# The middle of a hybrid decoder layer rewoven: residual stream kept in DRAM, memory norm and gates inside the input projection, two pairs of weight slots, the sample group inside the banded blocks

## The chip, the cores and the metric

The kernel runs on one core of one Trainium2 chip. The metric is the device time of one execution in microseconds (us), median of several runs. TensorE is called PE in the profile, VectorE DVE, ScalarE ACT, GpSimd POOL and SyncE SP. "tile m" below is an output tile of 128 features for all tokens.

## The reference

One decoder layer in float32 (D = 1024) for 1024 prompt tokens and 64 sample tokens (8 sequences of 8), with the same weights; the kernel puts the samples' 64 columns ahead of the prompt's, so T = 1088.

```
x  = x + 0.5 * swiglu(rmsnorm(x, g_ffn1), w1_gate, w1_up, w1_down)     # D_FF = 2816
h  = rmsnorm(x, g_mix);  [u | gate | q | k | v] = h @ w_in             # 512+512+512+128+128
conv = causal depthwise conv of width 4 over u
r, i = sigmoid(block_diag(w_a) conv + b_a), sigmoid(block_diag(w_i) conv + b_i)
a = exp(-8 r softplus(-lam));  b = sqrt(1 - a^2) * i * conv;  h_t = a_t h_{t-1} + b_t
lru_out  = rmsnorm(h * gelu(gate), g_lru_out)
attn_out = rmsnorm(attend(rope(q), rope(k), v, sink), g_attn_out)      # window 128, 8 heads, 2 kv heads
x  = x + concat(lru_out, attn_out) @ w_out
x  = x + softmax((rmsnorm(x, g_xattn) @ w_cq) mk^T / 16) mv @ w_co     # 4 heads, 256 memory tokens
       # prompt: mk, mv = rmsnorm(mem, g_mem) @ w_ck, @ w_cv;  samples: cached mk, mv
x  = x + 0.5 * swiglu(rmsnorm(x, g_ffn2), w2_gate, w2_up, w2_down)
y  = rmsnorm(x, g_final)
```

Besides y the outputs are mk, mv of the prompt, the last keys and values of the window, the convolution's last inputs and the LRU's last states.

## The kernel before

Activations lie with features on the partitions and tokens along the free dimension, in three chunks `CH = [(0, 288), (288, 512), (800, 288)]`. A product of the large weights is made of three matmuls in float32r: hi x hi, hi x lo and lo x hi of operands that are split into a high and a low part (`three`, L552 to L554). ACT writes the high part of activations (`hi_parts`, L1018), VectorE the low part (`lo_parts`, L1315). Weights come in pairs of 128x1024 tiles, 27 in all between the two FFNs (7 of w_in, 8 of w_ck and w_cv in turn, 4 each of w_out, w_cq, w_co), by one DMA per tile on SP's queue (`load_pairs`, L366) into `w_raw[0]` and `w_raw[1]`; GpSimd splits a tile in eight operations of 256 columns (`split_short`, L452 and L453) into the slot's `w_hi`, `w_lo`. There is one such pair of slots.

Input projection. Tile m uses slot m % 2 and PSUM banks 3s, 3s+1, 3s+2, one for each chunk; TensorE starts chunk c of tile m when VectorE has taken that chunk of tile m - 2 (`scaled_take`, L1412, which multiplies by the inverse RMS). VectorE does the convolution of LRU tile ct (L1482, L1489) between the takes of tiles 3 to 7; ACT copies its result over u (L1083). Ahead of tiles 8, 9, 10 and 11 TensorE does six float32 matmuls of the block-diagonal gate weights (`lru_gates`, L737) into banks 6 and 7 in turn, each waiting for ACT's sigmoid (L1092) of the one two before. ACT follows with tanh, exp and square root, VectorE with `lru_gated` (L1501 to L1505) and `lru_scan` (L1511 to L1522); all four LRU tiles share the buffers t_conv, t_a and t_b. ACT's gelu of all gate tiles (L1101) comes with the first of them.

Behind tile 12 come the sum of squares of the LRU output (`sum_squares`, L578), behind tile 13 that of the memory; VectorE does mean, reciprocal (L1302) and the multiplies of the memory norm (L1544), and only then the last take. GpSimd scales the LRU output (L505), four operations of 1088 columns.

Bands. The prompt is worked in eight blocks of 128 tokens. Per block TensorE does the scores (L780), turns the probabilities (`turn_p`, L794), rotates q and k for the block after the next (`rotate`, L768 and L769), does the two tiles of a memory pair (`memory_tile`, L552 to L554 with memn) and weighs the values (`weigh`, L802). VectorE adds the mask (L1587), takes the maxima (L1592), does the rope (L1572 to L1583), takes memory tiles and results out of PSUM (L1277) and normalizes (L1601); ACT does the exponentials (L1119) and copies the turned probabilities (L1131). A memory pair p is multiplied in block p; its weights are split once the pair before has left the slots. The scores of block b+1 are issued at the head of block b. Behind block 6 the samples' rotation, in block 7 their scores, and behind block 7 their turn and weighing (L896, L897) are done, then the attention norm and the output projection.

In SBUF the bands' tables, the rope's buffers and the split memory lie where the split activations `act_hi` and `act_lo` were; x keeps its own 34,816 bytes per partition all the time. The cross attention, its projection and the second FFN follow.

## Time and profile before

| | us |
|---|---|
| median of 3 runs | 2483.44 |
| lowest and highest | 2481.18, 2485.8 |
| the profiled execution | 2480.83 |
| its span (first to last instruction) | 2479.0 |

The span is taken by the hardware profiler. A line of a group names the line of the kernel, the engine and the operation, what it writes and reads, and its shape; behind it stand the busy time and the mean length of one in ns. The idle time in brackets or behind a bar is that of the engine just before the instruction, with what ended it. Matmuls are pipelined, so the length of one is longer than the distance from one to the next: the distance of 0.12 us for 256 columns is what it costs. The granted clock is TensorE's, as a share of 2.4 GHz; 0.5 is 1.2 GHz. The stages: first FFN to 823 us, input projection to 1028, prologue of the bands to 1069, bands to 1217, the samples' tail to 1230, attention norm with the first output tile to 1268, output, query and cross attention to 1670, second FFN and final norm to the end.

### The profile page before, as it was taken

Reading aid. Unit: us, or ns where it says so; the run is one execution under the profiler, and the core shown is the slowest. Engines: PE = TensorE matmul, PEld = TensorE weight load, DVE = VectorE, ACT = ScalarE, POOL = GpSimd, SP = SyncE. Lnnn points to the kernel's source line nnn. Section 1 sums busy time; section 2 is a strip of 40 time slices with the busy share of each in tenths; the row PEclk is TensorE's granted clock in tenths of the full one; section 3 lists DMA queues with packets and bytes.
Section 4 is the critical chain, followed back from the end, with each engine's and each line's share of the span. In section 5 each row is a group of like instructions: output and inputs, shape, how many; then the busy total and the mean of one; then the engine's idle time right before and its main releaser. Section 6 shows DMA issues by size and latency. Waiting matters only on the chain.

```text
span 2479.0 us, 35690 instructions
## 1 busy us (share of the span) xinstructions
PE 2333.8 (94%) x13994; PEld 2070.5 (84%) x13994; DVE 1431.7 (58%) x1864; ACT 444.1 (18%) x908; POOL 1029.9 (42%) x717
## 2 busy tenths in 40 slices
PE   6999999999999999688789989999999999999997
PEld 5899998999998887556578977889998999999896
DVE  7755555655555775876454324447655655565564
ACT  5111100110110416233322013231000000000002
POOL 2543443434433164546635430344434434344333
PEclk9999999999999999899889999999999999999998
DMA  4111101111010010201211134011011110110102
GB/s 142 69 40 45 47 20 51 51 51 51 34 42 26 26 43 26 97 28 58 71 55 48 34 137 170 26 59 69 21 47 51 51 51 35 50 40 28 68 0 74
DMA packets 40285, 131.89 MB, mean 53 GB/s; under 512 B 5799, under 2 KB 11047, under 8 KB 37799
## 3 DMA queue, kind: packets, MB, share of 16 engines
q1 hardware_dynamic: 37280, 127.80, 14.8%
q10 hardware_dynamic: 2951, 3.35, 0.4%
q8 instruction: 36, 0.59, 0.1%
q14 instruction: 18, 0.15, 0.0%
HBM read 123.33 MB, written 7.81 MB: 53 GB/s over the span
## 4 chain that ended last, share of the span: by engine, by line
PE 85%; DVE 6%; POOL 5%; ACT 3%; issue 1%; DMA 1%; POOLq 0%; SPq 0%; DVEq 0%; ACTq 0%
PE ps L552 27%; PE ps L554 26%; PE ps L553 26%; POOL w_hi L452 2%; POOL w_lo L453 1%; PE ps L961 1%; PE ps L914 1%; DVE act_lo L1315 1%; DVE rstd L1302 1%; DVE mem_raw L1544 1%; PE ps L737 1%; PE ps L578 0%; ACT sq L1003 0%; DVE y L1825 0%; ACT act_hi L1018 0%
## 5 line engine op out<-in xcount | busy, mean ns | idle before, releaser
L552 PE MATMUL ps<-act_hi,w_hi 128*128 128x288 f32 (+1 forms) x1968 | 658.0, 334 | 48.0 <-DVE act_lo L1315 34.8
L553 PE MATMUL ps<-act_lo,w_hi 128*128 128x288 f32 (+1 forms) x1968 | 653.1, 332 | 0.0
L554 PE MATMUL ps<-act_hi,w_lo 128*128 128x288 f32 (+1 forms) x1968 | 652.6, 332 | 0.0
L552 PEld LDWEIGHTS ps<-act_hi,w_hi 128*128 128x128 f32 x1968 | 377.5, 192 | 81.9 <-issue 38.6
L553 PEld LDWEIGHTS ps<-act_lo,w_hi 128*128 128x128 f32 x1968 | 377.6, 192 | 29.6
L554 PEld LDWEIGHTS ps<-act_hi,w_lo 128*128 128x128 f32 x1968 | 377.0, 192 | 29.1
L452 POOL TENSOR_TENSOR w_hi<-w_raw,ones 128x256 fp32r<-128x256 f32 x216 | 193.9, 898 | 472.2 <-PE ps L554 440.0
L1358 DVE SCALAR_TENSOR_TENSOR x<-ps,x 128x288 f32<-128x288 f32 (+1 forms) x504 | 263.6, 533 | 188.0 <-PE ps L554 172.8
L552 PE MATMUL ps<-hid_hi,dn_hi 128*128 128x288 f32 (+1 forms) x1056 | 348.7, 330 | 3.6 <-issue 3.6
L554 PE MATMUL ps<-hid_hi,dn_lo 128*128 128x288 f32 (+1 forms) x1056 | 347.7, 329 | 0.0
L553 PE MATMUL ps<-hid_lo,dn_hi 128*128 128x288 f32 (+1 forms) x1056 | 347.7, 329 | 0.0
L552 PE MATMUL ps<-act_hi,up_hi 128*128 128x288 f32 (+1 forms) x1056 | 347.6, 329 | 0.0
L554 PE MATMUL ps<-act_hi,up_lo 128*128 128x288 f32 (+1 forms) x1056 | 347.5, 329 | 0.0
L553 PE MATMUL ps<-act_lo,up_hi 128*128 128x288 f32 (+1 forms) x1056 | 347.5, 329 | 0.0
L1351 DVE TENSOR_TENSOR hid_lo<-hid_t,hid_hi 128x288 fp32r<-128x288 f32 x132 | 329.7, 2549 | 0.4
L443 POOL TENSOR_TENSOR w_hi<-w_raw,ones 128x1024 fp32r<-128x1024 f32 x42 | 102.0, 2428 | 506.8 <-PE ps L554 490.6
L1326 DVE TENSOR_TENSOR gate_t<-ps,rstd 128x288 f32<-128x288 f32 x132 | 70.0, 532 | 375.7 <-PE ps L554 375.1
L443 POOL TENSOR_TENSOR dn_hi<-w_raw,ones 128x1024 fp32r<-128x1024 f32 x22 | 52.9, 2406 | 396.1 <-PE ps L554 325.2
L552 PEld LDWEIGHTS ps<-hid_hi,dn_hi 128*128 128x128 f32 x1056 | 199.9, 189 | 19.2 <-issue 4.0
L554 PEld LDWEIGHTS ps<-hid_hi,dn_lo 128*128 128x128 f32 x1056 | 199.7, 189 | 16.0
L553 PEld LDWEIGHTS ps<-hid_lo,dn_hi 128*128 128x128 f32 x1056 | 200.0, 189 | 15.3
L553 PEld LDWEIGHTS ps<-act_lo,up_hi 128*128 128x128 f32 x1056 | 198.5, 188 | 16.0
(244 smaller groups left out, 2934.3 us busy)
## 6 DMA issues: line engine op xcount, KB each, us to landing
w_raw<-in_w_ffn SPq DMA_DIRECT2D x66, 512.0 KB, 3.7
w_raw<-in_w_plain SPq DMA_DIRECT2D x54, 512.0 KB, 3.6
ff_raw_up<-in_w_ffn SPq DMA_DIRECT2D x44, 512.0 KB, 4.4
ff_raw_down<-in_w_ffn SPq DMA_DIRECT2D x22, 512.0 KB, 6.4
ck_T<-in_ck SPq DMA_DIRECT2D x8, 1024.0 KB, 7.7
cv_n<-in_cv SPq DMA_DIRECT2D x8, 1024.0 KB, 4.9
x<-in_x SPq DMA_DIRECT2D x2, 1152.0 KB, 11.0
x<-in_x SPq DMA_DIRECT2D x1, 2048.0 KB, 12.0
```

Of the source, the lines that this page charges most:

```text
L443: steps.done(pool.tensor_tensor(hi[:, :, :], raw[:, :, :], one, ALU.mult))
L452: steps.done(pool.tensor_tensor(hi[:, r, :], raw[:, r, :], one, ALU.mult))
L453: ins = pool.tensor_tensor(lo[:, r, :], raw[:, r, :], hi[:, r, :].bitcast(F32), ALU.subtract)
L552: pe.matmul(out, wh, ah, start=(first and n == 0), stop=False)
L553: pe.matmul(out, wh, al, start=False, stop=False)
L554: ins = pe.matmul(out, wl, ah, start=False, stop=end)
L737: pe.matmul(ps[:, 6 + n_ % 2, 0:n], bd[:, ct, j // NC, :], mix[:, M_U + ct, o:o + n], start=True, stop=True).then_inc(lru_mm, 1)
L914: pe.matmul(ps[:, h // 2, (h % 2) * NM:(h % 2 + 1) * NM], xq_b[:, 2 * h + d, :], mem_kT[:, 2 * h + d, :], start=(d == 0), stop=(d == 1))
L961: ins = pe.matmul(ps[:, 6 + kt // 4, (kt % 4) * P:(kt % 4 + 1) * P], mem_v[:, mt, kt * P:(kt + 1) * P], xp_T[:, mt, kt // 2, :], start=(mt ...
L1326: dve.tensor_tensor(gate_t[:, o:o + n], ps[:, c, 0:n], rstd[:, o:o + n], ALU.mult)\
L1351: dve.tensor_tensor(hid_lo[s][:, o:o + n], hid_t[:, o:o + n], hid_hi[s][:, o:o + n].bitcast(F32), ALU.subtract).then_inc(f["hid_lo"], 1)
L1358: dve.scalar_tensor_tensor(out=x[:, m, o:o + n], in0=ps[:, DOWN_BANKS[n_ % 8], 0:n], scalar=0.5, in1=x[:, m, o:o + n], op0=ALU.mult, op1=A ...
```

## The change

- The memory's load and norm move to the front of the input projection: the sum of eight squares becomes three adds on VectorE, TensorE's sum comes ahead of tile 3, the multiplies ahead of the take of tile 3.
- x is written to DRAM behind the first FFN (one DMA) and read back in eight (one for each feature tile) behind the last band; the residual add of output tile m waits for its piece. In the meantime the split memory, the tables, the rope's buffers, the convolution's buffer and a second set of t_conv, t_a and t_b lie in its place.
- The gate matmuls of LRU tile ct come chunk by chunk behind the chunks of tiles 5, 7, 8 and 9. VectorE's and ACT's orders are rewritten to fit, with the convolutions in one buffer of their own and the multiply by the gate as a step of its own.
- The first rotation comes inside tile 13; the LRU's reciprocals move behind the first rope, with the takes of tile 13 between them.
- A second pair of weight slots, `kw_hi2[1]` and `kw_lo2[1]`, lies in the place of the activations; memory pair p uses pair p % 2. Pair 0 is multiplied ahead of block 0, pair b+1 in block b, none in block 7. The scores of block b+2 are issued at the end of block b. ACT takes one of a pair's two tiles out of PSUM. The blocks are written out, no longer in a loop.
- GpSimd scales the LRU output in quarters, one tile behind each of the pairs 3 to 6.
- The samples' rotation comes ahead of memory pair 0, their values, scores, turn and weighing behind blocks 0, 1, 3 and 4, in banks 4, 5 and 7.

The diff, cut to its core (buffers first, then SP, GpSimd, TensorE, ACT and VectorE):

```diff
+GATE_TILES = {5: 0, 7: 1, 8: 2, 9: 3}
+        memn_hi = at("memn_hi", [P, KT, NM], X0, F32R)
+        memn_lo = at("memn_lo", [P, KT, NM], X0 + 8192, F32R)
+        TAB0 = X0 + 16384
+        SET0 = (TAB0, P0 + IN_T * ROW)
+        t_conv = [at(f"t_conv{v}", [P, T], SET0[v]) for v in range(2)]
...
+        kw_hi2 = [w_hi2, here("kw_hi2", [P, 2, KT, P], F32R)]
+        kw_lo2 = [w_lo2, here("kw_lo2", [P, 2, KT, P], F32R)]
...
+            sp.wait_ge(f["dn_mm"], FI * NC * KT)
+            sp.dma_start(mem_raw[:, :, :], t_in["mem"]).then_inc(mem_in, 16)
+            sp.wait_ge(f["dn_ev"], 8 + FI * NC * KT)
+            sp.dma_start(t_in["x_keep"], x[:, :, :]).then_inc(x_kept, 16)
             load_pairs(1, 3)
...
+            sp.wait_ge(lru_h, 3)
             for dst, src in ((rotm, "rotm"), (rope_cos, "cos"), (rope_sin, "sin"), (ident, "ident")):
...
+            load_pairs(PAIR_KV + 1, PAIR_OUT + 2)
+            sp.wait_ge(pv_mm, NB)
+            sp.wait_ge(stored, 16 * 7)
+            for m in range(KT):
+                sp.dma_start(x[:, m, :], t_in["x_keep"][:, m, :]).then_inc(x_back[m], 16)
+            load_pairs(PAIR_OUT + 2, PAIR_CO)
...
+            for p in range(1, NB):
+                for s in range(2):
+                    if p == 1:
+                        pool.wait_ge(w_mm[1], groups_before(PAIR_KV))
+                    elif p % 2:
+                        pool.wait_ge(mem_mm, 2 * (p - 2) + 2)
+                    else:
+                        pool.wait_ge(mem_mm, 2 * (p - 2) + s + 1)
+                    split_plain(s, PAIR_KV + p, p % 2)
+                if 3 <= p < 3 + LT:
+                    lru_scale(p - 3)
...
+            def lru_gates(ct, c):
+                if c == 0:
+                    pe.wait_ge(conv_back, ct + 1)
...
+                for w in range(2):
+                    n_ = ct * 2 * NC + 2 * c + w
+                    if n_ >= 2:
+                        pe.wait_ge(lru_ev, n_ - 1)
+                    pe.matmul(ps[:, 6 + w, 0:n], bd[:, ct, w, :], mix[:, M_U + ct, o:o + n],
                               start=True, stop=True).then_inc(lru_mm, 1)
+            for m in range(2, IN_T - 1):
+                if m == 3:
+                    pe.wait_ge(ssq_ev, SUM0["mix"] + NC)
+                    sum_squares("mem", [(0, NM)], 1, mem_sq[:, 0, :])
+                if m in GATE_TILES:
+                    tile("in", m // 2, m % 2, m * NC, after=lambda c: lru_gates(GATE_TILES[m], c))
+                else:
+                    tile("in", m // 2, m % 2, m * NC)
+            pe.wait_ge(lru_ev, 2 * NC * LT)
+            sum_squares("lru", CH, 2 * LT)
...
             def rotate(b):
+                if b:
                     pe.wait_ge(rot_ev, b)
+                    pe.wait_ge(vt_ev, max(b - 1, 1))
+                    pe.wait_ge(kv_ev, max(b * 2 - 1, 3))
...
+            def block_step(b):
+                s = b % 2
+                pe.wait_ge(p_done, b + 1)
...
+                turn_p(b, s, 0)
+                if b + 2 < NB:
+                    rotate(b + 2)
+                turn_p(b, s, 1)
...
+                if b + 1 < NB:
+                    memory_tile(b + 1, 0)
+                weigh(b, 0)
+                if b + 1 < NB:
+                    memory_tile(b + 1, 1)
+                weigh(b, 1).then_inc(pv_mm, 1)
+                if b == 0:
+                    sample_values()
+                elif b == 1:
+                    sample_scores()
+                elif b == 3:
+                    sample_turn()
+                elif b == 4:
+                    sample_weigh()
+                if b + 2 < NB:
+                    scores(b + 2)
+                if b + 1 < NB:
+                    turn_v(b + 1)
+            tile("in", PAIR_KV - 1, 1, (IN_T - 1) * NC, after=rotate_first)
+            pe.wait_ge(g_ev["in"], 6 + 13 * NC + 1)
             scores(0)
+            sample_rotate()
+            pe.wait_ge(memn_lo_done, 1)
+            pe.wait_ge(rot_ev, 1)
+            memory_tile(0, 0)
+            memory_tile(0, 1)
+            pe.wait_ge(g_ev["in"], 6 + 3 * IN_T)
+            turn_v(0)
             rotate(1)
+            scores(1)
...
+            act.wait_ge(mem_in, 16)
+            act.activation(mem_sq[:, :, :], mem_raw[:, :, :], ACT.Square).then_inc(sq_done, 1)
+            rms("mem", [(0, NM)], of=mem_rstd)
+            act.wait_ge(mem_normed, 1)
+            act.wait_ge(x_kept, 16)
+            act.activation(memn_hi[:, :, :], mem_raw[:, :, :], ACT.Copy).then_inc(memn_hi_done, 1)
+            conv_copy(0)
+            for c in range(NC):
+                gates(0, c)
+            conv_copy(1)
+            decay(0)
+            conv_copy(2)
+            input_scale(0)
+            for c in range(NC):
+                gates(1, c)
+            conv_copy(3)
+            decay(1)
+            gates(2, 0)
+            gates(2, 1)
+            input_scale(1)
+            gates(2, 2)
+            decay(2)
+            gates(3, 0)
+            act.wait_ge(g_ev["in"], 6 + 8 * NC)
+            act.activation(mix[:, M_G:M_G + LT, :], mix[:, M_G:M_G + LT, :], ACT.Gelu_apprx_tanh)\
+               .then_inc(gate_gelu, 1)
+            gates(3, 1)
+            gates(3, 2)
+            input_scale(2)
+            decay(3)
+            input_scale(3)
...
+            convolve(0)
+            take_in(4)
+            convolve(1)
+            convolve(2)
+            take_in(5)
+            lru_gated(0)
+            take_in(6)
+            convolve(3)
+            lru_scan(0)
+            take_in(7)
+            lru_gated(1)
+            lru_scan(1)
+            take_in(8)
+            lru_times_gate(0)
+            lru_times_gate(1)
+            lru_gated(2)
+            take_in(9)
+            lru_scan(2)
+            lru_gated(3)
+            take_in(10)
+            lru_scan(3)
+            lru_times_gate(2)
+            lru_times_gate(3)
+            take_in(11)
...
+            rope_read(0)
+            rope(0, 0, steps)
+            for c, (o, n) in enumerate(CH):
+                dve.wait_ge(rms_done, SUM0["lru"] + c + 1)
+                dve.reciprocal(lru_rstd[:, o:o + n], lru_rstd[:, o:o + n]).then_inc(rstd_done, 1)
+                take_in(13, [c])
...
+            def block_step(b):
+                s = b % 2
+                if b + 1 < NB:
+                    add_mask(b + 1, 1 - s, masks[:, 2 - s, :])
+                    if b + 2 < NB:
+                        rope_read(b + 2)
+                    maxima(b + 1, 1 - s, steps)
+                    take_memory(b + 1, 0)
+                    if b + 2 < NB:
+                        rope(b + 2, s, steps)
+                    stage_v(b + 1)
+                    probabilities(b + 1, 1 - s, steps)
+                take_result(b)
...
+                    if stage == "out":
+                        dve.wait_ge(x_back[m], 16)
```

ACT's helpers in the diff: `conv_copy` is the copy of a convolution over u, `gates` the two sigmoids of one chunk, `decay` tanh and exp, `input_scale` the square root. VectorE's `convolve(ct)` waits for `conv_copy(ct - 1)`, since the convolutions now share one buffer.

## Rows read from the trace of the kernel before

**Rows 1.** The page's busy shares: engine, busy us, share of the span, instructions

```profile
PE 2333.8 (94%) x13994; PEld 2070.5 (84%) x13994; DVE 1431.7 (58%) x1864; ACT 444.1 (18%) x908; POOL 1029.9 (42%) x717
```

**Rows 2.** Windows by stage: us, each engine busy, clock, DMA share, GB/s

```profile
826.00:928.00 102.00, 100.71 (x584) 91.21 (x585) 73.38 (x104) 21.15 (x33) 49.95 (x57) 0.97 0.13 42
928.00:1028.50 100.50, 94.14 (x488) 76.00 (x486) 66.54 (x75) 54.96 (x62) 41.97 (x49) 0.97 0.12 38
1028.50:1069.40 40.90, 12.34 (x43) 7.34 (x41) 33.23 (x39) 7.91 (x21) 16.30 (x12) 0.58 0.27 93
1069.40:1217.00 147.60, 122.66 (x779) 87.43 (x779) 98.44 (x138) 50.11 (x152) 98.60 (x115) 0.97 0.20 58
1217.00:1229.70 12.70, 11.04 (x72) 8.82 (x72) 1.02 (x3) 1.06 (x2) 9.79 (x14) 0.69 0.23 61
1229.70:1268.40 38.70, 21.80 (x81) 17.23 (x82) 32.59 (x54) 19.74 (x36) 0.03 (x1) 0.70 0.09 35
```

**Rows 3.** Waits of TensorE, 815 to 1275: us in total, times, longest

```profile
PE ps L768 <- DVE mix L1412: 18.1, 1, 18.1
...
PE ps L552 <- POOL w_lo L453: 17.5, 10, 3.6
...
PE ps L780 <- DVE k_r L1583: 5.2, 2, 4.0
```

**Rows 4.** VectorE in order of time, 892 to 904: start, us, line, operation

```profile
892.03 0.46 DVE L1412 TENSOR_TENSOR mix<-ps,rstd 128x288 f32<-128x288 f32 x1 [0.59 <-PE ps L554]
...
902.44 1.05 DVE L1412 TENSOR_TENSOR mix<-ps,rstd 128x288 f32<-128x288 f32 x2
...
903.96 0.46 DVE L1412 TENSOR_TENSOR mix<-ps,rstd 128x288 f32<-128x288 f32 x1 [0.47 <-PE ps L554]
```

**Rows 5.** TensorE in order of time, first gate group, its first two matmuls

```profile
927.63 1.50 PE L737 MATMUL ps<-mix,bd 128*128 128x288 f32 x4
```

**Rows 6.** VectorE in order of time, reciprocals and memory norm behind the projection

```profile
1015.96 6.96 DVE L1302 RECIPROCAL lru_rstd<-lru_rstd 128x288 f32<-128x288 f32 x3
...
1031.46 13.94 DVE L1544 SCALAR_TENSOR_TENSOR mem_raw<-mem_raw,cst,acc 128x256 f32<-128x256 f32 x8
```

**Rows 7.** GpSimd in order of time, the LRU scale

```profile
1034.62 10.49 POOL L505 TENSOR_TENSOR mix<-mix,lru_rstd 128x1088 f32<-128x1088 f32 x4
```

**Rows 8.** Windows in which the DMA queues are full: keys in, results out

```profile
2472.00:2476.00 4.00, 0.73 (x4) 0.48 (x3) 3.23 (x8) 0.00 (x0) 0.00 (x0) 0.50 1.06 378
...
1466.00:1470.00 4.00, 1.84 (x5) 1.51 (x6) 2.11 (x5) 2.01 (x10) 0.00 (x0) 0.70 0.99 415
```

**Rows 9.** Groups by line and shape, 1069 to 1217: busy us, mean ns

```profile
L452 POOL TENSOR_TENSOR w_hi<-w_raw,ones 128x256 fp32r<-128x256 f32 x58 | 59.1, 1019 | 68.8 <-PE ps L554 68.8
...
L453 POOL TENSOR_TENSOR w_lo<-w_raw,w_hi 128x256 fp32r<-128x256 f32 x57 | 42.4, 743 | 4.5
...
L1119 ACT ACTIVATE s_m<-s_m,st 128x256 f32<-128x256 f32 x56 | 27.7, 495 | 15.6 <-DVE st L1595 15.6
...
L1601 DVE TENSOR_TENSOR s_m<-s_m,st 128x2048 f32<-128x2048 f32 x8 | 20.6, 2575 | 0.3
...
L1587 DVE TENSOR_TENSOR s_m<-ps,masks 128x2048 f32<-128x2048 f32 x7 | 16.0, 2280 | 0.1
...
L1592 DVE TENSOR_REDUCE st<-s_m 128x8 f32<-128x2048 f32 x7 | 15.9, 2273 | 0.0
```

**Rows 10.** TensorE in order of time, two blocks' first turns, a wait between

```profile
1086.42 1.09 PE L794 MATMUL ps<-ident,s_m 128*128 128x128 f32 x8
...
1090.74 0.35 PE L552 MATMUL ps<-w_hi,memn_hi 128*128 128x256 f32 x1 [1.02 <-POOL w_lo L453]
...
1102.77 1.09 PE L794 MATMUL ps<-ident,s_m 128*128 128x128 f32 x8
```

**Rows 11.** GpSimd in order of time, a long operation of a split

```profile
1100.44 2.79 POOL L452 TENSOR_TENSOR w_hi<-w_raw,ones 128x256 fp32r<-128x256 f32 x1
```

**Rows 12.** VectorE in order of time, the first normalizing, GpSimd idle

```profile
1067.02 2.29 DVE L1601 TENSOR_TENSOR s_m<-s_m,st 128x2048 f32<-128x2048 f32 x1
```

More of the change, by code:

```diff
@@ L305, in build @@
         mem_in = sem("mem_in")
+        x_kept = sem("x_kept")
+        x_back = [sem(f"x_back{m}") for m in range(KT)]
         kvc_in = sem("kvc_in")
@@ L690, in ffn_layer, with tile @@
                 last(f)
-            def tile(stage, p, s, n0, feed=None):
+            def tile(stage, p, s, n0, feed=None, after=lambda c: None):
                 pe.wait_ge(w_split[s], p + 1)
@@ new lines, in sample_weigh @@
+            def sample_weigh():
+                pe.wait_ge(s_pt_ev, 3)
+                pe.wait_ge(kv_ev, 2 * 6 + 1)
+                for b in range(NS):
+                    for kv in range(KVH):
+                        t, j = kv * 2 + b // 4, b % 4
+                        r = slice(kv * HD, kv * HD + HD)
+                        out = ps[r, 7, 256 + b * 32:256 + (b + 1) * 32]
+                        pe.matmul(out, v_c[:, b, r], pcs_T[:, t, 32 * j:32 * j + 32], start=True, stop=False)
+                        ins = pe.matmul(out, vs_n[:, b, r], pns_T[:, t, 32 * j:32 * j + 32], start=False, stop=True)
+                ins.then_inc(s_pv_mm, 1)
@@ L1137, in _, with sample_exps @@
+            def sample_exps():
+                act.wait_ge(s_nmax, 1)
+                for t in range(4):
+                    act.activation(ss_m[:, t, :], ss_m[:, t, :], ACT.Exp, bias=st4[:, 1, t:t + 1], scale=HD ** -0.5,
+                                   accum_out=st4[:, 4, t:t + 1])
+                act.activation(st4[:, 3, :], st4[:, 2, :], ACT.Exp).then_inc(s_exp, 1)
             act.sem_inc(pt_ev, 1)
+            take_memory(0, 0)
             exps(0, 0)
             take_v(0, 0)
-            with act.Fori(0, NB // 2 - 1) as i:
-                block_step(i * 2, 0)
-                block_step(i * 2 + 1, 1)
@@ L1691, in _ @@
+            for b in range(NB):
+                block_step(b)
             dve.wait_ge(stored, 16 * 7)
@@ L1725, in plain_residual @@
                     take(s, pair0, s)
-                with dve.Fori(1, KT // 2) as i:
-                    for s in range(2):
-                        take(i * 2 + s, i + pair0, s)
+                if stage == "out":
+                    for i in range(1, KT // 2):
+                        for s in range(2):
+                            take(i * 2 + s, i + pair0, s)
+                else:
+                    with dve.Fori(1, KT // 2) as i:
+                        for s in range(2):
+                            take(i * 2 + s, i + pair0, s)
                 dve.wait_ge(g_ev[stage], 6 + NC * KT)
```

574 lines of the change are left out of this document (269 added, 305 removed).

## The prediction

> **What bounds the kernel now.** The page's busy shares come first [rows 1]: TensorE is busy in 94% of the span. So matmuls bound the kernel wherever they are fed, and a change that takes few of them away can win only in holes. The windows by stage [rows 2] show how large these are. The first half of the input projection (826 to 928) has 1.3 us of TensorE idle; the half with the gates (928 to 1028.5) has 6.4; the prologue of the bands (1028.5 to 1069.4) has 28.6 of 40.9, at a mean granted clock of 0.58, so mostly at the 1.2 GHz level; the eight bands (147.6 us) have 24.9; the sample group's tail takes 12.7 us at 0.69; the norm after it has 16.9 of 38.7. The waits of TensorE [rows 3] name the holes that are reached here: 18.1 us for the last tile's take, which on VectorE stands behind the memory norm; 17.5 us in ten waits for GpSimd's weight splits; 5.2 us in two waits of the scores for the rope.
>
> **Input projection, tiles 8 to 13.** A tile takes 11.93 us (its take to that of the next [rows 4]). 100.5 us for six tiles leaves 100.5 - 71.6 = 28.9 us for the four gate groups, the LRU sums and stalls. Of a gate group's six matmuls the first two (chunks of 288 and 512) take 1.50 us [rows 5]; a third of 288 adds about 0.5, so six cost 4.0 (bounds 3.0, and 6.6, which is all of the 28.9 less the sums). Spread over three chunks they don't wait for sigmoids: the bank that each needs was emptied a chunk (3 to 5 us) ago. Four groups: 16.0. The LRU sums stay at an estimated 2.6; a memory sum of 0.5 and a rotation of 1.1 are new here. 28.9 - 20.2 = 8.7, of which stalls get 1.7: **7 us** (bounds 0 and 12).
>
> The stalls would come from VectorE's order. convolve(2) waits for ACT's copy of tile 1, which now stands behind the gates of tile 5, and the take of tile 5 stands behind convolve(2). A convolution with its copies is 9.9 us (892.5 to 902.4 [rows 4]). Tile 5 starts at 892, its gates end at 908, ACT has copied by 910, the convolution ends at 920, and tile 7 wants the bank at 920: under 1 us lost. Later VectorE waits some 7 us for the gelu, which stands on ACT behind the first gates of tile 9. As a load: VectorE had 73.4 + 66.5 us in both halves [rows 2]; 7.0 of reciprocals [rows 6] go to the prologue, the memory norm adds about 14: 147 in 192 us. Followed in order, it ends the adds for the LRU sums at 1000, and TensorE wants them at 1002.6. This slack of 3 us carries the part.
>
> **The memory norm.** Its eight multiplies took 13.94 us [rows 6], while GpSimd ran splits and the LRU scale [rows 7] without a gap. Now they lie in tile 3, beside at most one split: I take 7 us (0.9 each; bounds 3 and 14), and 2.3 each for the three adds in place of the reduction, for mean and reciprocal, and for the low part. Tiles 2 to 4 cover all of it, since VectorE has only 1.4 of takes in each 11.9 us there; without that cover the convolutions start later by as much and the 3 us are gone.
>
> **x to DRAM and back.** 4.46 MB each way. The queues moved 415 GB/s in and 378 GB/s out [rows 8], so 11 to 12 us, behind 3 us for the memory's 1 MB. The write starts at 827 with the last take, ends at about 842, and the weights of pair 1, queued behind it on SP, land by 845. Their slot is free at 842, TensorE needs the split at 856, a split is 6 us: 5 us remain. Cost 0 (bounds 0 and 5). The way back starts with the end of the last band, 1.5 us for each of eight pieces; the first output tile is taken over 20 us later, and the weights behind it on the queue (the third pair) are wanted later still. Cost 0.
>
> **Prologue.** Gone are the 18.1 us and the slow work behind them. After tile 13 (at about 1020 now) VectorE is still at the reciprocals with the takes between them; it starts on the scores about 3 us after the last matmul. Then one chain: mask 2.3, maximum 2.3 and small ones 0.6, eight exponentials of 0.5, the turn of the values 0.6, rotation 1.3 and rope 2.6 for block 1 (behind the exponentials, since the rotation waits for the copy of the first values; the rows bound a rope by 4.0 [rows 3]), normalizing 2.9 [rows 9]: 16.6. With 1 us for the clock, the first turn is 20.5 us after tile 13 and no longer 40.9: **20.4 us** (bounds 14 and 25). The sample's rope lies beside the exponentials, memory pair 0 in a hole of TensorE.
>
> **Bands.** From one block's first turn to the next's is 16.35 us, of which 1.02 is a wait for GpSimd [rows 10]: 15.3 us where the weights are there in time. Yet eight blocks took 147.6 us, as the next pair's split had to wait for the slots of the last. With two slot pairs GpSimd starts a block ahead. Now: block 0 with a cold clock 15.5, and its scores 2.2; six blocks 91.8, less 3.0 of rotation and scores that have no successor; block 7, without a memory pair, 7.6; the sample's four pieces 12 (the tail's 12.7 [rows 2] less its waits, plus its scores); friction 3. Sum 129: **18 us** (bounds 5 and 24).
>
> What must keep up. GpSimd: sixteen operations a pair, 1.02 on average for one half and 0.74 for the other [rows 9], are 14.1 us, 11.8 without VectorE's company; at shorter blocks I take 15.3. Four blocks add an LRU scale of 2.65 [rows 7]. From 1025: 12.5 + 6 x 15.3 + 10.6 = 115, pair 7 is ready at 1140; TensorE wants it 5.4 us into the turns of block 6, at 1148. VectorE: mask, rope read, maximum, exponentials and normalizing of the next block are 15.5 us from its scores, and TensorE comes for them after 17.1: 1.6 us of slack.
>
> **The sample's tail.** The 12.7 us between the last band and its result [rows 2] go, a take of 0.7 stays: **12 us** (bounds 9 and 12.7). The norm behind it keeps its chain and its cold clock.
>
> **Sum.** 7 + 20.4 + 18 + 12 = 57.4. The profiled execution took 2480.83 us (span 2479.0 and 1.8 around it), 2.6 under the median of the runs. 2480.8 - 57.4 + 2.6 = **2426 us**.
>
> **A rule against it.** One operation of GpSimd takes 2.79 us, where the mean of its line is 1.02 [rows 9, 11], and normalizing 2.58 on average [rows 9] where it takes 2.29 with GpSimd idle [rows 12]. The Trainium skill, "SBUF — State Buffer", section "SBUF: two separate sides", says that a VectorE operation with two SBUF inputs and a GpSimd operation take one port pair in turn, each for its whole length. By that rule, the trace agrees in these rows, a pair would cost GpSimd its 11.8 and VectorE's 4.2 of such work (2.3 of normalizing, the rest rope), 16.0, and pair 7 would come at 1144, still 4 us ahead: the sum stays.
>
> **Rivals.**
> First, VectorE sets the pace of the bands. For it: a slack of 1.6 us, and GpSimd now splits in all of a block and not in two thirds (98.6 of 147.6 [rows 2]); some nine operations of VectorE in a block read SBUF twice and can each meet one of 0.73, 0.4 on average, so 3.3 to 3.6 us, 2 beyond the slack. Against: 12.3 us of VectorE's work in 15.3. Over seven blocks 14 us: 2440. GpSimd at 17 us a pair would give the same.
> Second, the input projection turns into a convoy: each take of tiles 5 to 12 is late by 2 us behind a convolution or a scan. For it: VectorE and ACT each wait for the other in a strict order. Against: 147 in 192 us. The 7 us go and 8 more: 2441. Both together: 2455.
> Third, slower: the write of x runs far below the rate of the rows. The weights of tile 2 are behind it, and so is the memory's high part. The write has 12 + 5 us before TensorE waits; all beyond that is TensorE idle, and it eats the gain above 75 us, so under 60 GB/s. At 50 GB/s (89 us) it costs 72: 2498. For it: no row shows 4.46 MB in one write. Against: 378 GB/s of output [rows 8].
>
> **How the numbers follow.** The forecast has 0.63 (its own range 2417 to 2435), the first rival 0.17, the second 0.12, both together 0.04, the third 0.03, no change at all 0.01. Downward, 2411 holds 5 us more in the prologue, 6 in the bands and 4 in the projection, out of their bounds; upward both single rivals are in, with 9 us on top for the prologue's upper price: 2450. About 0.2% (5 us) can be told from no change. Faster 0.96, same 0.01, slower 0.03.
>
> **What would show it.** Tile 13 ends near 1020, the first turn comes near 1040; from one block's first turn to the next's 15 to 16 us, with no wait for GpSimd above 1 us; the last band ends near 1168, output tile 0 near 1207; the DMA share is near 1 for 12 us after 828. Wrong would be: waits of the projection's tiles for VectorE's takes over 5 us in all (second rival), a wait for the normalized scores in every block (first), a hole ahead of tile 2 (third).

## The result, and the profile after

The changed kernel takes 2420.55 us (median of four runs, 2418.85 to 2422.93), the one before 2482.44 us beside it: ratio 0.975, 95% interval 0.9738 to 0.9761, faster. The forecast was 2426 us, its range 2411 to 2450. On another chip the changed kernel took 2421.56 us (five runs, ratio 0.9754, interval 0.9741 to 0.9768).

The profiled execution has a span of 2417.1 us, 61.9 less than before. First the line of busy shares of its page; the line before is [rows 1].

```profile
PE 2317.7 (96%) x13994; PEld 2064.9 (85%) x13994; DVE 1432.2 (59%) x1858; ACT 449.6 (19%) x918; POOL 1052.5 (44%) x729
```

Just as many matmuls, but 16.1 us less of TensorE's busy time (its mean granted clock is 0.983, before 0.973); the rest of the gain, some 46 us, is holes. The windows by stage of the changed kernel (columns as in [rows 2], whose first four and last lines they answer):

```profile
826.00:928.00 102.00, 100.76 (x570) 89.95 (x571) 79.99 (x110) 36.45 (x49) 50.93 (x55) 0.97 0.27 96
928.00:1017.50 89.50, 89.50 (x506) 77.40 (x504) 73.79 (x91) 44.44 (x49) 60.54 (x50) 1.00 0.17 55
1017.50:1041.40 23.90, 14.96 (x91) 11.74 (x90) 19.55 (x27) 5.97 (x20) 21.09 (x25) 0.79 0.41 132
1041.40:1168.70 127.30, 121.55 (x801) 87.00 (x799) 98.03 (x123) 53.67 (x161) 107.08 (x127) 0.96 0.24 69
1168.70:1207.60 38.90, 20.73 (x74) 16.06 (x75) 32.38 (x52) 19.85 (x36) 0.00 (x0) 0.78 0.34 132
```

Against [rows 2] the second half of the projection is 11.0 us shorter, the prologue 17.0, the bands 20.3, and the samples' tail of 12.7 is gone; the norm behind it is 1.1 longer (output tile 0 is taken 38.8 us after its start, 37.7 before). That makes 59.9 of the 61.9. The last lines of this section say where most of the other 2 lies.

The waits of TensorE from tile 13's end to the last band (line, waited for, us in total, times, longest); they answer [rows 3]:

```profile
PE ps L819 <- DVE k_r L1711: 4.8, 1, 4.8
PE ps L835 <- ACT p_T L1235: 3.2, 3, 1.4
PE ps L829 <- DVE mem_kT L1390: 3.2, 1, 3.2
PE ps L581 <- issue: 2.3, 2, 1.2
PE ps L581 <- POOL w_lo L478: 0.6, 1, 0.6
```

The wait for the last tile's take (18.1) is gone, of 17.5 us for GpSimd 0.6 is left. What stays is one 4.8 us wait for a rope, and one of 3.2 for a memory tile that VectorE takes late. The 0.6 lies in the prologue; in the bands TensorE never waits for GpSimd. The two waits put down to "issue" (1.24 us at 1078.12 and 1.10 at 1094.38, ahead of the memory pairs in blocks 2 and 3) are VectorE's as far as the order shows: `block_step` waits there for `rot_ev`, and VectorE's last reading of that rotation ends at 1078.01 and 1094.27; one experiment's profile names it at this place (`DVE rot_k`, 1.4 us). VectorE in the prologue, in order of time (start, us, line, operation):

```profile
1026.31 0.42 DVE L1756 TENSOR_TENSOR rot_q<-ps,rope_sin 128x256 f32<-128x256 f32 x1
...
1029.54 0.41 DVE L1390 TENSOR_SCALAR mem_kT<-ps 128x256 f32<-128x256 f32 x1
1033.34 0.69 DVE L1700 TENSOR_TENSOR rot_q<-ps,rope_sin 128x512 f32<-128x512 f32 x1 [3.39 <-PE ps L808]
...
1036.10 1.17 DVE L1710 TENSOR_TENSOR q_r<-q_r,rot_q 128x512 f32<-128x512 f32 x1
1037.19 0.81 DVE L1711 TENSOR_TENSOR k_r<-k_r,rot_k 128x128 f32<-128x128 f32 x1
...
1038.34 2.47 DVE L1729 TENSOR_TENSOR s_m<-s_m,st 128x2048 f32<-128x2048 f32 x1
```

The samples' rope (1026.31 to 1029.6) stands ahead of the take that TensorE needs; then VectorE itself waits 3.39 us for the rotation, whose matmuls run at the low clock; then come the rope and the normalizing. The late take costs nothing, though. The rotation waits for ScalarE's copy of the first values, and that copy stands directly behind the exponentials, when the turn of the values (1030.10 to 1030.40) is already done:

```profile
1030.47 0.26 ACT L1219 ACTIVATE v_n<-ps 128x128 f32<-128x128 f32 x1
...
1030.83 2.04 PE L807 MATMUL ps<-mix,rotm 128*128 128x512 f32 x2 [0.43 <-ACT v_n L1219]
```

The write of x, in windows, first the kernel before, in which nothing is written, then the changed one:

```profile
830.00:840.00 10.00, 10.00 (x50) 8.95 (x49) 9.26 (x16) 8.98 (x15) 0.00 (x0) 0.86 0.00 0
```

```profile
830.00:840.00 10.00, 10.00 (x50) 8.91 (x49) 9.29 (x16) 9.00 (x16) 0.00 (x0) 0.87 0.99 385
840.00:850.00 10.00, 9.57 (x56) 8.03 (x55) 8.64 (x9) 5.77 (x7) 5.82 (x8) 1.00 0.23 73
```

385 GB/s from SBUF to DRAM, and TensorE, VectorE and ScalarE as busy beside it as without it: no hole ahead of tile 2. The memory's multiplies, in tile 3, took 5.28 us in place of the 13.94 of [rows 6].

The last 2 us: in the last product of the kernel, behind a stop of 2.05 us that both have, TensorE of the kernel before fell to its lower level for seven matmuls (0.43 apart, later 0.23), that of the changed one did not. Before, then after:

```profile
2446.70 1.14 PE L640 MATMUL ps<-y_id,lrup 96*128 96x96 f32 x6 [2.05 <-DVE lrup L1820]
2447.55 0.78 PE L552 MATMUL ps<-hid_hi,dn_hi 128*128 128x512 f32 x1
```

```profile
2386.45 0.91 PE L669 MATMUL ps<-y_id,lrup 96*128 96x96 f32 x6 [2.05 <-DVE lrup L1975]
2387.14 0.48 PE L581 MATMUL ps<-hid_hi,dn_hi 128*128 128x512 f32 x1
```

Nothing there was changed. That is about 1.5 us of clock, and no property of the change: in the second profile of the changed kernel, with a span of 2418.6, the same matmuls run at the low level again. The rest, some 0.5 us, is not followed up.

### The profile page after: what moved, and what is told of

Its sections match the earlier page's. It is cut to its first block, busy times and chain, and to the rows that moved or that the text cites. A ratio compares the mean times of both kernels' runs of the same rounds, so it can differ in the third digit from the quotient of the medians.

```text
span 2417.1 us, 35425 instructions
## 1 busy us (share of the span) xinstructions
PE 2317.7 (96%) x13994; PEld 2064.9 (85%) x13994; DVE 1432.2 (59%) x1858; ACT 449.6 (19%) x918; POOL 1052.5 (44%) x729
## 4 chain that ended last, share of the span: by engine, by line
PE 92%; DVE 4%; ACT 2%; POOL 1%; issue 1%; DMA 0%; ACTq 0%; SPq 0%; DVEq 0%; POOLq 0%
PE ps L581 28%; PE ps L582 28%; PE ps L583 28%; PE ps L981 1%; PE ps L843 1%; PE ps L1028 1%; DVE act_lo L1428 1%; PE ps L819 1%; PE ps L769 1%; DVE rstd L1415 1%; PE ps L607 1%; PE ps L835 1%; ACT sq L1070 0%; ACT act_hi L1085 0%; DVE y L1980 0%
## 5 line engine op out<-in xcount | busy, mean ns | idle before, releaser
L583 PEld LDWEIGHTS ps<-act_hi,w_lo 128*128 128x128 f32 x1968 | 377.2, 192 | 28.9
L477 POOL TENSOR_TENSOR w_hi<-w_raw,ones 128x256 fp32r<-128x256 f32 x184 | 162.7, 884 | 388.4 <-PE ps L583 356.6
L468 POOL TENSOR_TENSOR w_hi<-w_raw,ones 128x1024 fp32r<-128x1024 f32 x42 | 101.9, 2426 | 507.9 <-PE ps L583 491.7
L582 PEld LDWEIGHTS ps<-hid_lo,dn_hi 128*128 128x128 f32 x1056 | 199.9, 189 | 15.1
L581 PEld LDWEIGHTS ps<-act_hi,up_hi 128*128 128x128 f32 x1056 | 198.9, 188 | 15.9
```

Of the source, the lines that this page charges most:

```text
L468: steps.done(pool.tensor_tensor(hi[:, :, :], raw[:, :, :], one, ALU.mult))
L477: steps.done(pool.tensor_tensor(hi[:, r, :], raw[:, r, :], one, ALU.mult))
L581: pe.matmul(out, wh, ah, start=(first and n == 0), stop=False)
L582: pe.matmul(out, wh, al, start=False, stop=False)
L583: ins = pe.matmul(out, wl, ah, start=False, stop=end)
```

## The experiments

All times are medians. "The changed kernel" is 2420.55 us; "the changed kernel beside it" is its run on another chip, 2421.56, together with two of the experiments ("More work for GpSimd" and the first kernel of "The prologue in another order"). The length of a block is taken from the second half of its first turn to that of the next block's. No experiment takes back the prologue's 17.0 us alone, with the memory norm and the take of tile 13: that part is read from the two traces only.

### One weight slot pair

```diff
-        kw_hi2 = [w_hi2, here("kw_hi2", [P, 2, KT, P], F32R)]
+        kw_hi2 = [w_hi2, w_hi2]          # kw_lo2 likewise
...
-                    elif p % 2:
-                        pool.wait_ge(mem_mm, 2 * (p - 2) + 2)
+                    if p % 2:
+                        pool.wait_ge(mem_mm, 2 * (p - 1) + s + 1)
```

> The changed kernel (2420.6 us), with the second weight slot pair taken away: all memory pairs are split into the first pair of slots, each as soon as the matmuls that read its predecessor are through. Theory (the forecast's term for the bands): the eight bands were stretched by waits for GpSimd's splits alone, 17.5 us in ten waits in the kernel before. They come back: 15 to 20 us, so 2436 to 2441 us, first turn to end of last weighing about 144 us in place of 127. Rival: the gain in the bands came from the new order of the blocks (written out, rotation two blocks ahead, samples inside); then under 5 us come back, below 2426 us.

Measured: 2440.98 us, ratio to the kernel before 0.9833 (0.9817 to 0.985): 20.4 us come back. Its waits for GpSimd:

```profile
PE ps L579 <- POOL w_lo L478: 14.6, 6, 6.3
```

The slot pair is what the bands' gain hangs on, and the rival (the new order) is out. 14.6 is waiting. Part of the rest is the clock: block 4, with the weighing in it, takes 35.3 us in place of 26.7, though its wait is 6.3; over the bands the granted clock is 0.90 there and 0.96 in the changed kernel.

### Gate groups in one piece

```diff
-                    tile("in", m // 2, m % 2, m * NC, after=lambda c: lru_gates(GATE_TILES[m], c))
+                    tile("in", m // 2, m % 2, m * NC)
+                    for c in range(NC):
+                        lru_gates(GATE_TILES[m], c)
```

> The changed kernel with each LRU gate group in one piece behind its tile, no longer two matmuls behind each chunk. Theory: a group in one piece waits for the sigmoids of its first chunks; four groups took 28.9 us less 2.6 of sums in the kernel before, 6.6 us each, against 3.6 woven: 10 to 12 us come back, 2431 to 2433 us. Rival: the projection's gain came from VectorE's order and from the memory norm being gone there; then un-weaving costs under 3 us, about 2423 us.

Measured: 2434.99 us, ratio 0.9811 (0.9795 to 0.9827): 14.4 us, a little above the theory's 10 to 12. TensorE in order of time at tile 9's group, the last, and the stage's waits:

```profile
966.89 1.13 PE L769 MATMUL ps<-mix,bd 128*128 128x288 f32 x4
969.47 1.98 PE L769 MATMUL ps<-mix,bd 128*128 128x512 f32 x4 [1.44 <-ACT t_a L1167]
977.00 2.29 PE L769 MATMUL ps<-mix,bd 128*128 128x288 f32 x4 [5.55 <-ACT t_a L1167]
```

```profile
PE ps L769 <- ACT t_a L1167: 8.4, 3, 5.5
```

The wait of 5.55 is ScalarE's order: the gelu stands behind the first gates of the last group, and the rest of that group waits for it. Woven in, a chunk of large matmuls lies between. 8.4 us of waits, four groups of 4.75 in place of 4.1 and a clock of 0.97 in place of 1.00 make up the difference. Without the weaving none of the projection's gain (11.0) is left. The 14.4 is not the weaving's worth alone, though: 5.5 of it is an order of ScalarE that was made for woven groups and stayed here.

### The samples behind the last band

```diff
-                if b == 0:
-                    sample_values()
-                elif b == 1:
-                    sample_scores()
...
+            sample_values()
+            sample_scores()
+            sample_turn()
+            sample_weigh()      # behind the last block; ScalarE and VectorE likewise
```

> The changed kernel with the four sample pieces (values, scores, turn, weighing) in one chain behind the last band. Theory: the matmuls (about 12 us in the blocks) only move, but each piece now waits for VectorE or ScalarE: mask and maxima, exponentials, normalizing, copies, with a falling clock. 10 to 14 us more, 2431 to 2435 us. Rival: the pieces cost in the blocks what they cost behind them, the same matmuls being only moved: under 3 us, about 2423 us.

Measured: 2436.06 us, ratio 0.9814 (0.9797 to 0.983): 15.5 us more, the theory's side and a little above its 10 to 14. The windows of bands, samples and norm:

```profile
1042.00:1161.20 119.20, 110.08 (x658) 78.21 (x657) 97.96 (x113) 50.05 (x149) 109.59 (x127) 0.96 0.25 72
1161.20:1184.00 22.80, 15.21 (x145) 12.00 (x144) 3.77 (x10) 3.84 (x12) 0.00 (x0) 0.63 0.01 2
1184.00:1222.50 38.50, 20.02 (x76) 15.47 (x75) 32.05 (x51) 19.78 (x36) 0.00 (x0) 0.73 0.34 133
```

and of its waits:

```profile
PE ps L582 <- POOL kw_lo L479: 5.7, 2, 5.0
PE ps L892 <- DVE ss_m L1772: 5.3, 1, 5.3
```

Two things are to be seen. The tail costs 22.8 us, 10 more than the one of [rows 2], which had part of its work beside block 7. And the bands become only 8.1 us shorter, though the pieces are gone from them: without them blocks 0 to 3 take 15.0 to 15.3 us each, and then TensorE waits 5.0 us for pair 7. At 15.0 us a block GpSimd doesn't keep up: in the changed kernel the splits of a pair take it 12.0 to 15.1 us, 14.0 on average, and the four LRU scales between pairs 3 and 7 another 16.1 in all. The samples' pieces in the blocks, above all the weighing in block 4, give it the time.

### The write of x three times

```diff
+            for i in range(2):
+                sp.dma_start(t_in[f"x_keep{i}"], x[:, :, :]).then_inc(x_kept, 16)
             sp.dma_start(t_in["x_keep"], x[:, :, :]).then_inc(x_kept, 16)
```

> The changed kernel with the write of x made three times (to three tensors in DRAM, one behind the other on the same queue), 34.8 us in place of 11.6. Theory (slower rival of the forecast): the write may take 17 us before TensorE waits for the weights behind it, all beyond is idle TensorE: 18 us more (13 to 23), 2434 to 2444 us, with a hole ahead of tile 2. Rival: the three writes overlap or the weights are not held up by them; then under 5 us.

Measured: 2434.61 us (2431.02 to 2439.19), ratio 0.9809 (0.9791 to 0.9827): 14.0 us. TensorE's waits for GpSimd's splits, this one and the prologue's 0.6:

```profile
PE ps L583 <- POOL w_lo L480: 13.6, 2, 13.0
```

One hole of 13.0 us ahead of tile 2, where the theory had 18 and named the range from 13. 23.2 us of writes were added, so the slack behind the single write was some 10 us, where the theory had 17 - 11.6 = 5.4. The slower rival of the forecast is real as a mechanism; by this estimate it decides from about 22 us of write on, and the write takes 11.6.

### More work for GpSimd

```diff
+                for i in range(4):
+                    pool.tensor_tensor(pool_pad[:, :], memn_hi[:, 0, :].bitcast(F32), ...).then_inc(pad_done, 1)
+                    pool.wait_ge(pad_done, (p - 1) * 4 + i + 1)
```

> The changed kernel with four more GpSimd multiplies of 128x256 elements behind each memory pair's split (results unused), each waited for: some 3.5 us a pair. Theory: GpSimd runs without idle, but ahead of TensorE: pair 7 is ready at 1139 and wanted at about 1154, 15 us of slack; six additions of 3.5 are 21, so some 6 us (2 to 10) come out, 2423 to 2431 us. Rival (the forecast's first, GpSimd paces the bands): every addition counts, 20 to 25 us, 2441 to 2446 us. Third way: lock or port contention with VectorE lengthens each block by about 1 us more: 8 us on top.

Measured: 2429.95 us, ratio 0.9786 (0.9771 to 0.9801): 8.4 us over the changed kernel beside it, for some 20 us of additions. TensorE waits for GpSimd once in the bands:

```profile
PE ps L586 <- POOL kw_lo L480: 9.4, 1, 9.4
```

It stands ahead of pair 5 (1110 to 1120), not pair 7 as the theory had it. In the changed kernel pair 5 is ready at 1106.72 and wanted at 1110.45, a lead of 3.7; four additions stand ahead of it, and 3.7 + 9.4 makes them 3.3 us each. So GpSimd does not pace the changed kernel, but its lead is smallest there, and what goes beyond it comes through once; the weighing behind it gives a new lead.

### The prologue in another order

The samples' rotation and rope go into tile 13, the last reciprocal into block 0, the first values' turn and block 1's rotation directly behind the first scores:

```diff
                     pe.wait_ge(rope_tab, 64)
+                    sample_rotate()
                     rotate(0)
...
             scores(0)
-            sample_rotate()
-            memory_tile(0, 0)
-            memory_tile(0, 1)
             turn_v(0)
             rotate(1)
+            memory_tile(0, 0)
+            memory_tile(0, 1)
             scores(1)
```

> The changed kernel with another order ahead of the bands: the samples' rotation and rope while tile 13 is still on TensorE, the last reciprocal of the LRU norm inside block 0, the turn of the first values and block 1's rotation directly behind the scores of block 0, memory pair 0 behind them. Theory: the first turn waits for one chain of VectorE and ScalarE (mask, maxima, rope of the samples, rotation and rope of block 1, normalizing), 23.8 us behind tile 13; taken off it are 1.4 us of reciprocal, 3.3 us of sample rope, and some 3 us of rotation at low clock and rope that now lie beside the exponentials: 7 us less (4 to 8), 2413 us (2412 to 2417). Rival: the blocks behind absorb it, since VectorE then has less slack and GpSimd's splits come as late as before: under 2 us, 2419 us.

> The changed kernel itself, on the same chip as the two others of this call: 2420.6 us, within 0.1%.

Measured: 2418.33 us, ratio 0.9744 (0.9731 to 0.9758), 3.2 us under the changed kernel beside it, with intervals that overlap: the theory's 7 (4 to 8) missed. The first turn comes at 1035.92, 5.4 us sooner than in the changed kernel's first profile and 4.3 sooner than in its second, but not before ScalarE's exponentials had waited for their table:

```profile
1026.68 0.38 ACT L1230 ACTIVATE mem_kT<-ps 128x256 f32<-128x256 f32 x1 [4.82 <-PE ps L583]
1027.08 1.28 ACT L1215 ACT_TABLE_LOAD   x1
1028.37 0.51 ACT L1215 ACTIVATE s_m<-s_m,st 128x256 f32<-128x256 f32 x1
```

The maxima were there at 1026.8; the load had been hidden at 1023.67 in the changed kernel. Of the 5.4 us 1.5 go at once: the first half of that turn and the rotation behind it run at the low clock, 3.7 us from the first half to the second in place of 2.2. Another 0.9 goes in the blocks. The next kernel takes the tile with VectorE, and puts the samples' values and block 2's rotation ahead of the first turn.

> The kernel of e6_prologue (2418.3 us) with three more moves ahead of block 0: VectorE, not ScalarE, takes the first memory tile, so that ScalarE's table load of 1.28 us no longer stands between that take and the exponentials; block 2's rotation and the turn of the samples' values go into TensorE's hole before the first turn. Theory: the exponentials began 2.0 us behind the maxima there, the values' turn is 1.0 us of block 0, the first rotation was waited for by VectorE for 1.75 us: first turn near 1034, and 3 to 4.5 us less than e6_prologue, 2414 to 2415.5 us. Rival (what e6_prologue hints at, where 4.6 us at the first turn had become 3.2 at the end): the blocks behind take it back, since VectorE or GpSimd is next; then under 1 us, 2417.5 us.

Measured: 2417.35 us (2412.65 to 2418.69), ratio 0.9733 (0.972 to 0.9747): 1.0 us less by the medians and 2.6 by the means of the runs, which overlap with those of the kernel before it. So time alone doesn't part the theory (3 to 4.5) from the rival (under 1); the profile has the last block's first turn 1.5 us sooner. Normalizing ended at 1034.6, but the turn waited until 1036.4 for ScalarE's copy of the samples' values; and behind it stood already GpSimd's pair 1, a wait of 1.1 us at 1040.8.

### The weighing between large matmuls

```diff
-                    memory_tile(b + 1, 0)
+                    memory_tile(b + 1, 0, sample_weigh if b == 4 else lambda n: None)
...
+                    if k < KT - 1 or j == 0:
+                        between(j * KT + k)      # 4 matmuls of 32 columns at every other k
```

In the changed kernel the weighing and the scores behind it look so (TensorE in order of time, block 4; the profile has two records for each of these matmuls, so 64 for the 32 of the code):

```profile
1122.10 0.30 PE L908 MATMUL ps<-pns_T,vs_n 8*64 8x32 f32 x2
...
1122.78 0.42 PE L907 MATMUL ps<-pcs_T,v_c 128*64 128x32 f32 x2
...
1129.78 3.58 PE L819 MATMUL ps<-k_r,q_r 64*128 64x256 f32 x16
```

> The changed kernel with the samples' weighing (64 matmuls of 32 columns) no longer in one piece behind block 4, but in eight portions between the matmuls of memory pair 5, into another bank, its result taken by ScalarE. Theory: in one piece it takes 9.8 us of a wholly busy TensorE, its pairs go from 0.23 to 0.35 us when the granted clock falls to its lower level, and the scores behind it take 3.58 in place of 2.0. Between large matmuls the clock stays up: 32 pairs of 0.23 are 7.4, scores 2.0, so 4 us less (3 to 6), 2416.6 us. Rival: the small matmuls between large ones cost their weight loads just the same and the clock falls for another reason: no gain, 2420.6 us, or some us more.

> Both of the two above in one kernel. Theory: they lie in different blocks, so the gains add: 7.5 to 10 us less than the changed kernel, 2411 to 2413 us. Rival: GpSimd's splits, which stand still in neither, come to set the pace when the blocks get shorter; then waits of TensorE for GpSimd return (more than 2 us in all), 2414 us or more.

Measured: alone 2421.41 us (2419.24 to 2424.91), ratio 0.9754 (0.974 to 0.9767), no gain, the rival; with both, 2414.40 us (2413.31 to 2415.12), ratio 0.9728 (0.9715 to 0.9741), 3 us less than the better prologue alone (the runs of the two overlap) and 6 to 7 us under the changed kernel. The theory had 7.5 to 10; the rival's time came, but not its waits, since TensorE waits 1.1 us for GpSimd and not over 2. The intervals of the two ratios just touch (0.9741 and 0.9738); their runs are apart (up to 2415.12, from 2418.85). No later kernel is faster beyond its spread. The windows 1120 to 1130 and 1130 to 1140, first of the kernel with the weighing alone (its slowest run, 2424.91 us), then with both:

```profile
1120.00:1130.00 10.00, 10.00 (x52) 7.25 (x53) 7.85 (x9) 0.00 (x0) 5.31 (x7) 0.76 0.17 54
1130.00:1140.00 10.00, 9.68 (x42) 5.27 (x42) 3.18 (x3) 1.73 (x4) 7.60 (x11) 0.73 0.12 21
```

```profile
1120.00:1130.00 10.00, 9.43 (x60) 6.24 (x58) 4.81 (x4) 1.96 (x4) 9.77 (x12) 1.00 0.29 83
1130.00:1140.00 10.00, 10.00 (x63) 7.62 (x64) 9.66 (x15) 5.56 (x19) 9.53 (x13) 1.00 0.27 76
```

In the first the clock fell all the same, some us later, and then large matmuls ran at half speed too: block 4 took 28.8 us in place of 26.7. In the second it stayed, and the block took 24.4. So the piece is worth 1 to 2 us where the clock holds (one piece behind block 4 takes that block 25.5 to 26.7 us in the profiles without a wait there) and loses 2 where it doesn't; the cause of its fall is not settled.

### What is next behind the prologue

```diff
             memory_tile(0, 0)
+            sample_values()
             memory_tile(0, 1)
```

> The kernel of e9_both (2414.4 us) with two small moves: the turn of the samples' values lies between the two halves of memory pair 0, so that the first turn no longer waits 1.75 us for ScalarE's copy of them, and of the samples' maxima only the mask stays in block 1, the rest (2.8 us of small operations beside GpSimd) goes behind block 2's rope, where VectorE waits for exponentials. Theory: GpSimd is next: pair 1 is split at 1040.0, and its half-pairs then follow each other without idle every 7.5 to 8 us; the 1.75 us at the first turn are lost again at memory pair 1 (the wait for GpSimd there grows from 1.1 to nearly 3 us), the 2.0 us of TensorE's gap in block 2 are won: 2412.5 us (2411.5 to 2414). Rival: VectorE's order is what counts, both are won: 2410.5 us. Third way: the small operations in block 2 delay its normalizing, and nothing is won.

Measured: 2413.93 us, but from 2412.29 to 2428.24; ratio 0.973 (0.9717 to 0.9743). The profile is of the slowest of the five. In it the first turn comes at 1033.54, 2.4 us sooner than in the kernel before it, and TensorE gives it back at pair 1:

```profile
PE ps L581 <- POOL kw_lo L478: 4.2, 1, 4.2
```

1.1 us had become 4.2 (the theory had nearly 3): GpSimd, whose pair 0 waits for the slot of the projection's last tiles and whose pair 1 starts at 1025.8 only, behind a wait for its weights, now bounds the prologue.

```diff
-                if 3 <= p < 3 + LT:
-                    lru_scale(p - 3)
+            for ct in range(LT):
+                lru_scale(ct)            # behind pair 7; from the kernel with both
```

> The kernel of e9_both (2414.4 us) with the four LRU scales of GpSimd, 2.9 us each between memory pairs 3 to 6, in one piece behind pair 7. Theory: memory pairs 4 to 7 come 3 to 12 us sooner, but TensorE did not wait for them, since the samples' pieces, above all the weighing in block 4, give GpSimd the time: the same within 1 us, 2414.4 us; the distances of blocks 2 and 3 stay at 17.2 us. Rival: GpSimd paces blocks 2 to 4 (17.2 us each, against 15.0 without the samples' pieces), and 2 to 4 us are won, 2411 us. In both the clock of TensorE in blocks 4 and 5 can move the time by some us.

Measured: 2419.19 us, from 2411.61 to 2425.44, ratio 0.9737 (0.9718 to 0.9757): in time inconclusive. The blocks tell it: GpSimd now idles before pair 7,

```profile
1126.48 0.72 POOL L477 TENSOR_TENSOR kw_hi<-w_raw,ones 128x256 fp32r<-128x256 f32 x1 [10.83 <-PE ps L583]
```

and blocks 1 to 4 take 16.9, 16.7, 17.0 and 24.4 us, against 16.9, 17.2, 17.2 and 24.4: at most 1 us was GpSimd's.

## Why the prediction was right, step by step

- **Input projection, 7 forecast, 11.0 measured.** The mechanism was right (un-weaving costs 14.4), the size low: a gate group woven in is 3.6 us net (1.13, 1.88 and 1.13 in three places, less their overlap) and not 4.0, and of the 1.7 us of stalls only 0.4 came, a wait for the adds. Part of the 28.9 us that the forecast started from was clock: 0.91 was granted from 948 to 988, behind two of the gate groups in one piece, and 1.00 in the changed kernel. Tile 13 ended at 1017.5, not 1020. VectorE's order went as followed: the wait before convolve(2), the take of tile 5 at 918.3, the wait for the gelu to 963, and the adds done at 1002.35 where 1000 was forecast and 1002.6 wanted.
- **Memory norm, 7 us in tile 3.** 5.28 for the multiplies. Nothing waited.
- **x to DRAM and back, 11 to 12 us, at no cost.** 385 GB/s out, 412 in the window 1171 to 1181 on the way back; TensorE as full beside the write as without it.
- **Prologue, 20.4 forecast, 17.0 measured: the mis-sized term.** From tile 13's end to the first turn it took 23.8 us, not 20.5. The chain is the forecast's, link by link: the samples' rope did lie beside the exponentials, and the rotation did wait for the copy of the first values behind them. Two of its links were too short. "Rotation 1.3 and rope 2.6": the rope took 4.7 us (1033.34 to 1038.0) beside GpSimd's splits, where 2.6 was entered from rows with GpSimd idle, and the rotation 2.5 at the low clock. The second profile of the changed kernel has 4.3 for the rope again but 1.5 for the rotation, so only the first is steady. Most of the rest is 0.4 in the small operations behind the maxima and 0.5 behind the normalizing, where block 1's scores took 3.37 us at the low clock in place of 2.00; against all this the forecast had 1 us for the clock. The bound of 4.0 for a rope stood in the text and wasn't taken. Two operations of a rope in the kernel before, with GpSimd idle, of which the changed kernel's lines at 1036.10 and 1037.19 above are the counterparts (1.17 and 0.81 us):

```profile
1064.00 0.69 DVE L1582 TENSOR_TENSOR q_r<-q_r,rot_q 128x512 f32<-128x512 f32 x1
1064.61 0.28 DVE L1583 TENSOR_TENSOR k_r<-k_r,rot_k 128x128 f32<-128x128 f32 x1
```

- **Bands, 18 forecast, 20.3 measured.** 127.3 us against 129. With a single slot pair 20.4 us come back. The block itself is 15.0 to 15.3 (the kernel with the samples behind shows it bare), as entered; the samples' pieces are 12.9 and not 12, and 1.6 more for the scores at low clock behind them; the 3 us of friction were too many. In the measure that the forecast named, from one block's first turn to the next's, the blocks took 16.2, 16.1, 16.4, 17.3, 26.2, 15.5 and 13.1 us: only block 5 lies in 15 to 16. Blocks 0, 1, 3 and 4 hold a sample piece, 2 and 3 a wait for VectorE, and block 6 has neither rotation nor scores behind it. Pair 7 was ready at 1139.3 (forecast 1140), wanted at 1152.0 (1148). That 1140 was met is luck: a pair took 14.0 us and not 15.3, and the four scales 16.1 and not 10.6.
- **Tail, 12 forecast, 12.7 measured,** as the pieces' cost stands in the bands.
- **The rivals.** GpSimd did not hold TensorE up in the bands, though it was busy 107 of 127 us, and a wait returned as soon as a pair cost 3.3 us more or the blocks took 15.0. VectorE did so for 1.2 and 1.1 us in blocks 2 and 3, by its late reading of the rotation, but never with the normalized scores. So the first rival was near. There was no convoy. The slow write did not come; tripled, it cost a hole where the text had it.

The terms' errors (+4.0, -3.4, +2.3, +0.7, -1.1) come to 2.5 us with their signs and to 11.5 without: that the sum lies so near is partly luck. Of the rest of the 5.4 us between 2426 and 2420.55, 1.0 is the kernel before, 2482.44 us beside the changed one where the forecast started from 2483.4, and most of the other 2 is the clock at the very end.

The rule on the shared port pair shows in single operations. Three tiny ones of the samples' maxima (128x4), first in the changed kernel, beside GpSimd, then with GpSimd idle, in the kernel with the samples behind:

```profile
1073.67 0.55 DVE L1776 TENSOR_TENSOR st<-st 128x4 f32<-128x4 f32 x1
1074.25 0.17 DVE L1777 TENSOR_SCALAR st<-st 128x4 f32<-128x4 f32 x1
1074.45 0.57 DVE L1778 TENSOR_TENSOR st<-st,cst 128x4 f32<-128x4 f32 x1
```

```profile
1166.08 0.16 DVE L1764 TENSOR_TENSOR st<-st 128x4 f32<-128x4 f32 x1
1166.27 0.17 DVE L1765 TENSOR_SCALAR st<-st 128x4 f32<-128x4 f32 x1
1166.48 0.16 DVE L1766 TENSOR_TENSOR st<-st,cst 128x4 f32<-128x4 f32 x1
```

By the Trainium skill, "SBUF — State Buffer", section "SBUF: two separate sides", the pair is locked for a whole instruction; the trace agrees: the two with two inputs took 0.4 us more, about half of a split's 0.73 us. The same lengthening, 0.5 us in each of the rope's four operations with two SBUF inputs, makes the 2 us that the forecast's rope lacked. The forecast had that rule at hand and worked out a pair by it, 16.0 us and pair 7 at 1144, which is more than the 14.0 and 1139.3 measured, but it did not ask what the rule does to the rope. Not all of it is so plain: a TENSOR_SCALAR on 128x8 (L1722) took 0.59 us at 1025.60, and 0.17 in the second profile of the same kernel.

## What to carry to other kernels

Give a producer that splits or stages weights a second slot before trying to make it faster: one pair of slots was worth 20 us here, at a producer that was busy no less afterwards (a faster one was not tried). Put small dependent work into the blocks of a busy loop, not behind it: the same matmuls cost 15.5 us more in a chain of their own. When such a stage is shortened, ask at once who comes next: here it was the producer's first start, and of 7 us forecast for a better prologue 3 arrived. Take a VectorE operation's length from rows in which GpSimd does what it will do beside it.

## What was not expected of the hardware

- TensorE's granted clock falls to its lower level while the engine is busy without a gap: 10.00 of 10.00 us busy and 0.64 granted in 1120 to 1130 of the changed kernel, where it ran the matmuls of 32 columns. The Trainium skill, "TensorE: Matmul & The Clock Gate", section "Part 1: The HAM clock gate (the "warmup" mystery)", has the clock follow how busy TensorE was; in this row, read by its busy column, the trace does not agree.
- Where it fell, large matmuls behind or between the small ones also ran at half speed (scores 3.58 in place of 2.00 us). The spread of one kernel goes with this: the last but one experiment took 2412.3 us at a mean granted clock of 0.987 and 2428.2 at 0.981, and 0.006 of 2412 us, an estimate of what the lower clock cost, is 14.5 of the 15.9.
- A single 4.46 MB write from SBUF to DRAM ran at 385 GB/s, at no cost to TensorE, VectorE or ScalarE beside it: in 830 to 840 they were busy 10.00, 9.29 and 9.00 us, and 10.00, 9.26 and 8.98 in the kernel before.
